# 94 matmuls on constants added to a two-layer decoder step: 14 behind the transposes of x, 80 ahead of the recurrent output projection

## What is computed

```python
def rglru_mixer(a, conv_buf, h0, w_in, w_conv, b_conv, w_ga, b_ga, w_gx, b_gx, lam, w_out):
    gate, xb = jnp.split(a @ w_in, 2, axis=-1)
    xc, new_buf = causal_dwconv(xb, conv_buf, w_conv, b_conv)
    r = jax.nn.sigmoid((block_diag(xc, w_ga) + b_ga).astype(jnp.float32))
    ig = jax.nn.sigmoid((block_diag(xc, w_gx) + b_gx).astype(jnp.float32))
    ...
    h_last, hs = lax.scan(step, h0.astype(jnp.float32), (jnp.swapaxes(a_t, 0, 1), jnp.swapaxes(b_t, 0, 1)))
    hs = jnp.swapaxes(hs, 0, 1).astype(a.dtype)
    y = (jax.nn.gelu(gate) * hs) @ w_out
    return y, new_buf, h_last.astype(a.dtype)
```

## Time and profile before

| | |
|---|---|
| runs | 679.82, 680.48, 681.27 us; median 680.48 |
| profiled execution | 684.84 us, its span 683.03 us |
| TensorE busy | 598.2 us (88% of the span) |
| VectorE, ScalarE, GpSimd busy | 480.5, 350.5, 275.8 us |
| mean granted clock of TensorE | 0.933 |

### The profile page before, as it was taken

One profiled execution on the slowest core, in us unless ns is written; L12 is line 12 of the kernel. 1 busy time (PEld: TensorE's weight loads), 2 busy tenths in 40 slices (PEclk: granted clock), 3 DMA queues, 4 the chain that ended last, 5 costly groups with the idle time before them and its releaser, 6 DMA issues.

```text
span 683.0 us, 12723 instructions
## 1 busy us (share of the span) xinstructions
PE 598.2 (88%) x5020; PEld 510.8 (75%) x5020; DVE 480.5 (70%) x876; ACT 350.5 (51%) x568; POOL 275.8 (40%) x275
## 2 busy tenths in 40 slices
PE   6869357369979999999999998948999999999995
PEld 5647246249867888888888887746888888888885
DVE  4569974576439888887865568797988778885442
ACT  6414204136427766665654458954776656663322
POOL 5843316127313354455400139983245545440001
PEclk9869759769999999999999999986999999999999
DMA  8833329913327876666876555542667666679601
GB/s 246 233 94 98 92 63 283 272 31 95 92 67 269 252 208 195 192 200 194 256 213 202 141 154 155 147 131 66 194 202 202 200 191 198 202 225 254 173 10 64
DMA packets 206076, 115.42 MB, mean 169 GB/s; under 512 B 5769, under 2 KB 202489, under 8 KB 205993
## 3 DMA queue, kind: packets, MB, share of 16 engines
q1 hardware_dynamic: 203601, 108.46, 56.1%
q0 software_dynamic: 2048, 5.79, 2.6%
q10 hardware_dynamic: 368, 0.35, 0.2%
HBM read 110.94 MB, written 3.90 MB: 168 GB/s over the span
## 4 chain that ended last, share of the span: by engine, by line
PE 56%; DVE 17%; issue 14%; POOL 5%; DMA 4%; ACT 4%; POOLq 1%; SPq 0%; ACTq 0%; DVEq 0%
PE acc L1263 16%; PE acc L1264 16%; PE acc L1265 16%; DVE w_lo L796 4%; DMA scratch<-q_rows 3%; POOL area L1593 3%; ACT w_hi L498 1%; DVE area L1179 1%; DMA pt<-in_page_table 1%; PE acc L1352 1%; DVE area L929 1%; DVE aL L803 1%; PE acc L1353 1%; PE acc L1354 1%; PE misc L1461 1%
## 5 line engine op out<-in xcount | busy, mean ns | idle before, releaser
L1263 PE MATMUL acc<-aH,w_hi 128*128 128x264 f16 (+1 forms) x1032 | 288.4, 279 | 1.1 <-DVE aL L803 0.8
L1264 PE MATMUL acc<-aL,w_hi 128*128 128x264 f16 (+1 forms) x1032 | 288.4, 279 | 0.0
L1265 PE MATMUL acc<-aH,w_lo 128*128 128x264 f16 (+1 forms) x1032 | 288.2, 279 | 0.0
L796 DVE SCALAR_TENSOR_TENSOR w_lo<-stage,w_hi 128x1024 f16<-128x1024 f32 (+1 forms) x179 | 235.0, 1316 | 52.8 <-ACT w_hi L498 52.2
L498 ACT ACTIVATE w_hi<-stage 128x1024 f16<-128x1024 f32 (+1 forms) x179 | 196.9, 1101 | 85.1 <-PE acc L1265 78.4
L1263 PE MATMUL acc<-zH,w_hi 128*128 128x264 f16 x440 | 121.5, 276 | 0.0
L1264 PE MATMUL acc<-zL,w_hi 128*128 128x264 f16 x440 | 121.4, 276 | 0.0
L1265 PE MATMUL acc<-zH,w_lo 128*128 128x264 f16 x440 | 121.4, 276 | 0.0
L1263 PEld LDWEIGHTS acc<-aH,w_hi 128*128 128x128 f16 (+1 forms) x1032 | 102.7, 99 | 19.2 <-issue 1.6
L1264 PEld LDWEIGHTS acc<-aL,w_hi 128*128 128x128 f16 (+1 forms) x1032 | 102.3, 99 | 17.6 <-issue 0.3
L1265 PEld LDWEIGHTS acc<-aH,w_lo 128*128 128x128 f16 (+1 forms) x1032 | 102.3, 99 | 16.3
(11 more groups left out here) (340 smaller groups left out, 742.4 us busy)
## 6 DMA issues: line engine op xcount, KB each, us to landing
stage<-in_w_ffn_up SPq DMA_DIRECT2D x88, 512.0 KB, 4.6
stage<-in_w_ffn_down SPq DMA_DIRECT2D x32, 704.0 KB, 5.0
stage<-in_w_attn_in SPq DMA_DIRECT2D x26, 512.0 KB, 4.3
stage<-in_w_rec_in SPq DMA_DIRECT2D x16, 512.0 KB, 4.0
stage<-in_w_attn_out SPq DMA_DIRECT2D x8, 512.0 KB, 3.7
stage<-in_w_rec_out SPq DMA_DIRECT2D x8, 512.0 KB, 3.7
scratch<-q_rows SPq DMA_DIRECT2D x8, 256.0 KB, 8.1
area<-in_x_prompt SPq DMA_DIRECT2D x2, 512.0 KB, 4.7
```

The costliest lines, as they stand in the source:

```text
L796: v.scalar_tensor_tensor(w_lo[:, s, 0:n, 0:cols], stage[:, s, 0:n, 0:cols], WSCALE, w_hi[:, s, 0:n, 0:cols], ALU.mult, ALU.subtract).then_ ...
L1263: t_.matmul(out, w_hi[:, s, c, 0:cols], xH[:, x0 + c, :], start=first and c == 0, stop=False)
L1264: t_.matmul(out, w_hi[:, s, c, 0:cols], xL[:, x0 + c, :], start=False, stop=False)
L1265: ins = t_.matmul(out, w_lo[:, s, c, 0:cols], xH[:, x0 + c, :], start=False, stop=last and c == n - 1)
```

## The change

A helper `keep_warm` is made of the loop over `ones`, and the 16 first calls go through it unchanged. Two uses are added: 14 calls into the third accumulator bank between the transposes of x and the first paired units; and, after the last gate unit, a wait for all 16 tanh of the gates and then 80 calls into bank `A`, ahead of the paired units of the recurrent output projection. The results of the calls are not read. Nothing else differs.

```diff
+            def keep_warm(out, n):
+
+                for _ in range(n):
+                    t_.matmul(out, ones[:], ones[:], start=True, stop=True)
+
...
             pe.wait_ge(ones_set, 1)
-            for _ in range(WARM):
-                t_.matmul(acc[:, 0, 0:P], ones[:], ones[:], start=True, stop=True)
+            keep_warm(acc[:, 0, 0:P], WARM)
             pe.wait_ge(const_in, 16)
...
+            keep_warm(acc[:, 2, 0:P], 14)
             units_together(0, 2, aH, aL, a_ready(0))
             for u in range(2, U_OUT + 1):
...
+            pe.wait_ge(gate_tanh, 2 * DC)
+            keep_warm(A[:, 0:P], 80)
             units_together(U_ROUT, 2, zH, zL, lambda c: pe.wait_ge(y_lo, c + 1))
             for u in range(U_ROUT + 2, U_ROUT + DC):
                 unit(u, zH, zL)
```

## The result

The changed kernel takes 685.14 us in the median (683.26 to 689.69, 22 runs), the kernel before 682.01 us (679.05 to 684.74, 22 runs on the same occasions). The ratio is 1.0053, with a 95% interval of 1.0037 to 1.0070: slower by 3.6 us, 2.5 to 4.8. The forecast was slower by 2.3, at 682.8 us with a range up to 684.6. The sign was right; the measured time lies 0.5 us above the range. Ratios and means leave out single executions that lie more than 1.5% above the fastest of their kernel; "all runs" and the counts of runs above 684 us take them in.

What follows compares the result with a forecast made beforehand. TensorE, full nearly everywhere from slice 11, was taken to bound the kernel, with GpSimd's indirect-load chain deciding early. Early calls 0 plus late calls +2.3 us gave 682.8 us, range 681.2 to 684.6.

Steps and rivals of the forecast that it cites:

- The calls' price, their end and the clock: Ahead of the recurrent output projection: 0.223 us a call, 80 taking 17.84 us to 470.08, TensorE's clock staying full.
- The rival of short calls: Late calls cost under 0.195 us each and end before 467.86: gain of 2.90, 677.6 us; chance 0.04.
- The loss at the second place: At the projection's paired units, the 80 calls overrun: next unit +2.22 us later, bounds 1.8 to 3.0, taken as 2.3.
- Nothing behind takes it up: After the paired projection units TensorE has no gap, so their delay reaches the kernel's end in full.
- The base: Kernel-before time used for the forecast: run median 680.48 us, 4.4 below the profiled sum; 0.1 allowed for spread of medians.
- So I cost this edit at nothing: GpSimd's chain hides it: The 14 early calls: first paired group ends near 20.4 instead of 23.0, hidden by VectorE's 5.81 us wait; 0 us.
- The early gain: Rival: the first paired group's earlier end moves the whole kernel, -0.3 us in sum, 680.2 us; chance 0.06.
- The clock was not lost: Rival at the projection: the calls don't hold the clock, which falls at 454.40; +5.1, 685.6 us; chance 0.03.

Runs made afterwards that it cites:

- only80: The changed kernel without its 14 early calls, against the kernel before: ratio 1.0034, mean +2.7 us.
- only14: The changed kernel without its 80 late calls, against the kernel before: ratio 0.9999, mean 0.0 us.
- n48: The changed kernel with 48 late calls in place of 80, against the kernel before: ratio 0.9984, mean -0.9 us.
- n160: The changed kernel with 160 late calls in place of 80, against the kernel before: ratio 1.0334, mean +22.8 us.
- again: The changed kernel itself measured once more, against the kernel before: ratio 1.0048, mean +3.4 us.
- early80: 80 calls at the early place in place of 14, no late calls, against the kernel before: ratio 1.0124, mean +8.7 us.
- n56: The changed kernel with 56 late calls in place of 80, against the kernel before: ratio 0.9969, mean -2.3 us.
- early4x512: 4 early calls of 512 columns in place of 14 of 128, no late calls, against the kernel before: ratio 1.0015.
- only14d: The 14 early calls alone, fourth sample, against the kernel before: ratio 1.0008.
- n70: The changed kernel with 70 late calls in place of 80, against the kernel before: ratio 1.0022, mean +1.3 us.
- only80b: The 80 late calls alone, second sample, against the kernel before: ratio 1.0022, all-runs mean 684.1 us.
- only80c: The 80 late calls alone, third sample, against the kernel before: ratio 1.0032, all-runs mean 684.1 us.
- only56: 56 late calls and no early ones, against the kernel before: ratio 0.9974, all-runs mean 679.3 us.
- only14b: The 14 early calls alone, second sample, against the kernel before: ratio 1.0039, all-runs mean 686.9 us.
- early40: 40 calls at the early place in place of 14, no late calls, against the kernel before: ratio 1.0127, all-runs mean 691.6 us.

## Why the prediction was right and wrong

**The calls' price, their end and the clock** were right: 0.2234 us a call, an end 17.87 us after the start, clock 1.00 throughout. The rival of short calls is out: 80 more cost 17.9 us more. So is, for calls of this type, the rule by which they would have been short (the Trainium skill, TensorE: Matmul & The Clock Gate, "Back-to-back issue gap").

**The loss at the second place** was right, +2.2 in this pair of traces, and its bounds of 1.8 and 3.0 nearly so. Over the nine traces without late calls the place takes 54.1, 53.9, 54.0, 53.9, 54.1, 53.0, 54.0, 54.0 and 52.8 us, 53.7 in the mean, where it is 56.3 or 56.4 with 80. That makes +2.6 in the mean and up to +3.5. My 2.3 was 0.3 too low: I gave the profiled execution, in which the old clock came back late, more weight than the middle of my own bounds.

**Nothing behind takes it up** was right: TensorE is 186.00 of 186.00 us busy after it too, and the last norm sum stands 190.4 or 190.5 us before the end in before, after, only80, only14, n48, n160 and again.

**The base** is the step that failed: "The median of the runs is 680.48, 4.4 lower, and I add the same difference there", with a range "widened by 0.1 for the spread of medians". The median of 22 runs is 682.01, 1.5 us higher. The measured 685.14 is 2.3 above the forecast: 1.5 are the base, 0.8 the change itself, +3.1 by the medians for +2.3. Single runs of the kernel before spread from 679 to 685, with a standard deviation of 1.7 us, so that the median of three of them scatters by over 1 us; the range had 0.1 for it, and 1.5 was needed. With the better base the forecast would have been 684.3 and the range 682.7 to 686.1, with 685.14 inside. None of this has to do with the mechanism.

**"So I cost this edit at nothing: GpSimd's chain hides it"** is in doubt, though its reason holds. The group did end 2 us earlier, the DMA and GpSimd did hide it, and early80 measures the very 5.8 us of cover. By the means, 3.6 us measured less 2.6 at the second place leave 1.0 us, twice its standard error at best. By the same account, against the mean place of 53.7 and early80's 7.3, the other kernels with early calls leave -0.2 (n48), 0.0 (n56, only14), 0.5 (early4x512), 0.7 (only14d), 0.8 (again), 0.9 (n70), 1.4 (early80) and 2.3 us (n160) in the quiet sets, and the 14 alone over 5 us in the two disturbed ones; those with late calls alone leave about nothing (only80 +2.7, and by all runs only80b +2.4 and only80c +3.0 for 2.6, only56 -2.5 for -2.3). The quiet traces show no loss ahead of the second place: it begins at 435.3 to 438.7 us, 436.7 in the mean, in the eight with the 14 calls, and at 437.3 and 438.5 in the two without early calls.

That runs are late more often with the early calls is shown for the disturbed sets. What the 1.0 us of the quiet ones is stays open: the same effect at a lower frequency, scatter, or something that grows with the late calls when both parts are there, as n48 and n56 against n70, the changed kernel and n160 would suggest; no run has 160 late calls without the early ones. How the early calls make TensorE's signals late stays open as well: the moved fetch goes with it, and the run meant to separate the two fell on a quiet occasion.

**The rivals.** The early gain did not reach the end. The clock was not lost with the 80 calls; it was with 48, by a pause that my sketch of 80 short calls, with 1.9 us of idle time, had let pass.

## What to carry to other kernels

Filler that keeps TensorE's clock up pays only as long as it ends with the wait that it fills, and it has to reach over the short waits that follow too: here 56 calls gave -2.3 us and 48 gave -0.9, while 80 alone gave +2.7, by an overrun of 5 us over what full clock gains. Price it from a row of the same instruction, then count from the end: last data, plus the work that may start only then. Don't put filler where another chain hides the gain, and don't take three runs for a base when the effect is 0.3%.

## What the runs showed of the hardware

- A pause inside a group cost the clock: 1.29 of 3.10 us busy, with one wait of 1.66, and TensorE was at 0.50 for the next 3.4 us (n48). With a wait of 0.21 us in the same place it stayed at 1.00 (n56).
- A float32 matmul of 128 columns is two records, and a call takes 0.2234 us at 2.4 GHz and about 0.427 at 1.2 GHz, where a 16-bit one of 264 columns takes 0.1127.
- On some occasions TensorE's matmuls and its semaphore updates come late between 15 and 34 us of this kernel, in the part where sixteen indirect loads and the first weight loads run: the pair's `unit_done` at 32.86 us (only14b) where it is at 20.41 (only14), and in only80c 11 us behind the matmul that raises it. ScalarE and VectorE wait for it, up to 15.1 us at a time (early40); GpSimd goes on. The same traces lack most of their semaphore records there (63 to 229 of some 650). In those two sets runs above 684 us are 19 of 24 with the 14 early calls alone and 18 of 76 without any.
